# Where the vector and weight work stands at the entry of the recurrence and of the second feed-forward block

## The chip, the core and the metric

The kernel runs on one core of one Trainium2 chip. The metric is the device time of one execution in microseconds (us); the time of a kernel is the median of several runs. Five engines work side by side, each through its own instruction list: TensorE (PE, the matrix products), VectorE (DVE), ScalarE (ACT), GpSimd (POOL) and SyncE (SP, which only starts transfers). They meet through semaphores.

## What is computed

One step of a small audio encoder: 1152 columns (1024 frames of a prompt and 8 streams of 16 frames) by 1024 features, in float32. Two layers, each with a mixer and a feed-forward block:

```python
for i in range(DEPTH):                       # DEPTH = 2
    h = rmsnorm(x, norm_mix_w[i])
    out = conv_module(h, ...) if i == 0 else hgrn2_mix(h, ...)   # hgrn2: gated recurrence
    x = x + out
    h = rmsnorm(x, norm_ffn_w[i])
    x = x + conv_ffn(h, ...)                 # up to 2 x 2816, 3-tap conv, silu gate, down
y = rmsnorm(x, norm_final_w)
# hgrn2_mix: q, f, v, g = split(h @ w_in); f goes through a sigmoid; 8 heads of 128;
# block-wise recurrence per head; normed, gated by silu(g); @ w_o
```

`rmsnorm` divides each column by the root of its mean square over the 1024 features.

## The kernel before, in words

Activations lie by features: `X` is 8 tiles (index m or k) of 128 partitions by 1152 columns. A float32 product is made of three passes over values cut in two: `XH` and `WH` hold rounded high parts, `XL` and `WL` what is left, and a tile product is XH·WH + XL·WH + XH·WL. One output tile of 128 features by 1152 columns is "a product": 8 values of k, three passes, three thirds of 384 columns (`NCH = 3`), so 72 matmuls, each third into a bank of its own of `BANKS` (PSUM). Two sets of three banks take turns; banks 6 and 7 (`MB`) take the column sums.

**Weights.** Each weight unit (128 by 1024) is loaded by SP and cut by POOL (`split(u)`: a touch of one element, L455, a copy to `WH`, L456, a subtraction to `WL`, L458). There are two slots, so `split(u)` waits until the product of unit u-2 is done, and the product of unit u waits for `w_split`.

**A norm at the entry of a block.** `X[m]` becomes final when DVE has added the last product's tile m (`add`, L1341 and L1343). ACT then writes `XH[m]` (`high`, L916) and the square of `X[m]` into one of two `SQ` buffers (L929); DVE writes `XL[m]` (`low`, L1215); POOL adds the square into `ACC` (`square(q0, m)`, L469 and L472). ACT's square m waits until POOL has taken square m-2. After all eight, PE sums `ACC` over features with a matrix of ones (`stats`, L560, three matmuls, one per third), ACT takes the roots (`rms`, L937), DVE their reciprocals (`rstd`, L1223, three of 384 columns). The scale is applied only when a product is read, so the first product of a block runs without it.

**Entry of the recurrence** (unit numbers from `U_HG`). PE makes the products F, Q and V of head 0 (`part`, L671): F in banks 0 to 2, Q in banks 3 to 5, V again in banks 0 to 2, for which DVE must have read F. The statistics stand after two values of k of Q. POOL cuts F's unit, adds all eight squares, then cuts Q's unit. DVE does the three reciprocals, reads F and Q (`projected`, L1496), then clears `SC` and turns the mask, loaded by ACT, to bytes (L1623, L1624).

**Entry of the second feed-forward block.** The eight output tiles of the recurrence (`U_WO` to `U_WO + 7`, PE L883) are added to `X` one after another, one product apart. POOL cuts all eight units and the first of the feed-forward block (`U_F1`), and only then starts on the squares. For this block ACT writes `XH[0]` to `XH[6]` after square 6, since the last output product still reads the old `XH`:

```python
if late is not None and m == KD - 1:
    for k in range(KD - 1):
        act.wait_ge(x_used, late + k + 1)
        high(k)
```

The entry of the first feed-forward block has the same form (eight products L538 of the convolution module's last matrix, then the block), but there POOL's code reads `split(U_PW2 + 2 + m)`, `square(Q_F0, m)` in turn.

Of the kernel before, what the change touches and what calls it, by code (L numbers as in the profile page):

```python
# [5 lines left out]
ALU = mybir.AluOpType  # L6
# [6 lines left out]
P = 128  # L13
# [4 lines left out]
KD = D // P  # L18
# [10 lines left out]
NCH = 3  # L29
# [16 lines left out]
U_HG = U_F0 + FFN_UNITS  # L46
U_WO = U_HG + HG_BIGS
U_F1 = U_WO + KD
# [9 lines left out]
M_N0, M_F0, M_HG = 0, 3, 6  # L58
# [5 lines left out]
Q_N0, Q_F0, Q_HG, Q_F1, Q_FIN = (KD * n for n in range(5))  # L64
# [46 lines left out]
def big_no(what, h):  # L111
    return BIGS.index((what, h))
# [48 lines left out]
def build(nc, d_w, d_x, d_par, d_taps, d_ffp, d_fhist, d_chist, d_state, d_const, d_mask,  # L161
          o_y, o_convp, o_convs, o_hgp, o_hgs, o_ffn):
    with ExitStack() as ctx:  # L163
# [3 lines left out]
        def sem(name):  # L167
            return ctx.enter_context(nc.semaphore(name))
# [3 lines left out]
        XH = sb("XH", [P, KD, T], F32R)  # L172
        XL = sb("XL", [P, KD, T], F32R)
        WRAW = sb("WRAW", [P, 2, 1024])
        WH = sb("WH", [P, 2, 1024], F32R)
        WL = sb("WL", [P, 2, 1024], F32R)
        RSTD = sb("RSTD", [P, T])
# [62 lines left out]
        FG = cut(T, of=HGA)  # L240
# [6 lines left out]
        SC = cut(TCH, P, of=HGA)  # L247
# [3 lines left out]
        VM = cut(NB, P, of=HGA)  # L251
        MASK = cut(LEVELS * P // 4, of=HGA).bitcast(U8).rearrange("p (l c) -> p l c", l=LEVELS)
# [19 lines left out]
        def big_place(what, h):  # L272

            p = 1 if (what, h) == ("Q", 0) else 0
            return PS[:, p * NCH:(p + 1) * NCH, 0:CW]
# [19 lines left out]
        w_split = sem("w_split")  # L295
# [3 lines left out]
        mb_free = sem("mb_free")  # L299
# [7 lines left out]
        mask_in = sem("mask_in")  # L307
# [22 lines left out]
        g_hi = sem("g_hi")  # L330
        g_lo = sem("g_lo")
        a_full, a_free = sem("a_full"), sem("a_free")
        s_full, s_free = sem("s_full"), [sem("s_free0"), sem("s_free1")]
        kept, o_rdy = sem("kept"), sem("o_rdy")
        f_sig = sem("f_sig")
# [7 lines left out]
        def third(k):  # L343
            return slice(k * CW, (k + 1) * CW)
# [21 lines left out]
        def full_big(eng, what, h):  # L366

            eng.wait_ge(a_full, big_no(what, h) + 1)

        def emptied_big(eng, what, h):  # L370

            eng.wait_ge(a_free, big_no(what, h) + 1)
# [67 lines left out]
        @block.gpsimd  # L440
        def _(pool):
            def split(u, i=0, per=0, used=None):


                s = u % 2
                pool.wait_ge(raw_ld[s], lin(i, 8 * per, raw_count(u)))
                if U_HG <= u - 2 < U_WO:
                    pool.wait_ge(a_full, u - 2 - U_HG + 1)
                elif used is None and u >= 2:
                    used = (unit_tile(u - 2) + 1, 0)  # L450
                if used is not None:
                    pool.wait_ge(ps_full, lin(i, used[1], used[0]))

                one = WRAW[:, s, 0:1]
                nc.gpsimd.tensor_tensor(PAD, one, one, ALU.mult)  # L455
                nc.gpsimd.tensor_copy(WH[:, s, :], WRAW[:, s, :]).then_inc(w_hi, 1)  # L456
                pool.wait_ge(w_hi, lin(i, per, u + 1))
                nc.gpsimd.tensor_tensor(WL[:, s, :], WRAW[:, s, :], WH[:, s, :].bitcast(F32),  # L458
                                        ALU.subtract).then_inc(w_split, 1)

            def squares(q0):

                for m in range(KD):
                    square(q0, m)

            def square(q0, m):
                pool.wait_ge(sq_rdy, q0 + m + 1)
                if m == 0:
                    nc.gpsimd.tensor_copy(ACC, SQ[:, 0, :]).then_inc(sq_add, 1)  # L469
                else:  # L470
                    pool.wait_ge(sq_add, q0 + m)
                    nc.gpsimd.tensor_tensor(ACC, ACC, SQ[:, m % 2, :], ALU.add).then_inc(sq_add, 1)  # L472

            def loop(first, times, u, per_u, per_t):

                with pool.Fori(first, times) as i:
                    for k in range(per_u):
                        v = u + k + per_u * first
                        before = unit_tile(v - 2) + 1 - per_t * first
                        assert unit_tile(v - 2 + per_u) + 1 - per_t * (first + 1) == before  # L480
                        split(u + k, i, per_u, (before, per_t))

            def ffn(u0):

                for u in range(u0 + 2, u0 + 7):
                    split(u)
                loop(1, FGROUPS - 1, u0 + 1, 6, 12)
                for u in range(u0 + 1 + 6 * (FGROUPS - 1), u0 + FFN_UNITS):
                    split(u)

            split(0)
            split(1)
            for u in range(U_PW1 + 2, U_PW1 + 6):
                split(u)
            loop(1, (KD - 2) // 2, U_PW1 + 2, 4, 6)
            for u in range(U_PW2 - 2, U_PW2):
                split(u)
            split(U_PW2)
            split(U_PW2 + 1)

            for m in range(KD - 1):
                split(U_PW2 + 2 + m)
                square(Q_F0, m)
            square(Q_F0, KD - 1)
            split(U_F0 + 1)
            ffn(U_F0)

            split(U_HG)
            squares(Q_HG)
            split(U_HG + 1)  # L510
            for u in range(U_HG + 2, U_F1):
                split(u)
            split(U_F1)
            squares(Q_F1)
            split(U_F1 + 1)
            ffn(U_F1)
            squares(Q_FIN)
# [3 lines left out]
        def _(pe):  # L521
# [129 lines left out]
            def part(what, h, k0, k1, lows=None):  # L651

                a = big_no(what, h)
                s = (U_HG + a) % 2
                if k0 == 0:
                    pe.wait_ge(w_split, U_HG + a + 1)
                    if (what, h) == ("F", 0):
                        emptied(pe, T_HG - 2)
                    elif (what, h) == ("Q", 0):
                        emptied(pe, T_HG - 1)  # L660
                    elif (what, h) == ("V", 0):
                        emptied_big(pe, "F", 0)
                    else:
                        pe.wait_ge(a_free, a)
                for k in range(k0, k1):
                    if lows is not None:
                        pe.wait_ge(x_lo, lows + k + 1)
                    wh, wl = WH[:, s, k * P:(k + 1) * P], WL[:, s, k * P:(k + 1) * P]
                    for q, (w, x) in enumerate(((wh, XH), (wh, XL), (wl, XH))):
                        for c in range(NCH):  # L670
                            ins = nc.tensor.matmul(big_place(what, h)[:, c, :], w, x[:, k, third(c)],  # L671
                                                   start=(k == 0 and q == 0), stop=(k == KD - 1 and q == 2),
                                                   skip_group_check=True)
                if k1 == KD:
                    ins.then_inc(a_full, 1)

            def take(what, h):

# [84 lines left out]
                ins.then_inc(s_full, 1)  # L763

            part("F", 0, 0, KD, lows=P_HG)
            part("Q", 0, 0, 2)
            stats(M_HG, Q_HG)
            part("Q", 0, 2, KD)
            part("V", 0, 0, KD)
            scores(0, 0)  # L770
            part("G", 0, 0, 3)
            values(0)
# [136 lines left out]
        def _(act):  # L909
# [23 lines left out]
            def rms(m0):  # L933

                for c in range(NCH):
                    act.wait_ge(mb_full, m0 + c + 1)
                    A(RSTD[:, third(c)], MB[:, (m0 + c) % 2, 0:CW], ACT.Sqrt, bias=EPSC, scale=1.0 / D  # L937
                      ).then_inc(mb_free, 1)
# [159 lines left out]
                act.dma_start(XKEPT[m], X[:, m, :]).then_inc(kept, 16)  # L1098

            split_x(Q_HG, P_HG, C_MIX1, x_kept)  # L1100
            rms(M_HG)

            act.wait_ge(ffn_out, 16)
            act.dma_start(VM, d_mask).then_inc(mask_in, 16)

            def load_state(h):
                act.dma_start(SIN, d_state[h]).then_inc(state_in, 16)
# [90 lines left out]
        def _(dve):  # L1198
# [3 lines left out]
            def mine():  # L1202

                dve.wait_ge(dv, dc.now())
# [14 lines left out]
            def rstd(m0):  # L1219

                for c in range(NCH):
                    dve.wait_ge(mb_free, m0 + c + 1)
                    dc.inc(V.reciprocal(RSTD[:, third(c)], RSTD[:, third(c)]))  # L1223
                mine()
# [266 lines left out]
            def projected(what, h, dst):  # L1491

                full_big(dve, what, h)
                if what == "G":
                    mine()
                V.tensor_tensor(pieces(dst), big_place(what, h), pieces(RSTD[:]), ALU.mult).then_inc(a_free, 1)  # L1496
# [117 lines left out]
                V.tensor_tensor(XL[:, k, :], X[:, k, :], XH[:, k, :].bitcast(F32), ALU.subtract  # L1614
                                ).then_inc(x_lo, 1)

            rstd(M_HG)

            dve.wait_ge(ffn_out, 16)
            projected("F", 0, FG)  # L1620
            projected("Q", 0, QFS[0])
            dve.wait_ge(mask_in, 16)
            dc.inc(V.memset(SC, 0.0))  # L1623
            dc.inc(V.tensor_copy(MASK, VM))  # L1624
            mine()

            forget(0)
            key(0)
# [174 lines left out]
```

## Time and profile before

| | |
|---|---|
| median of 3 runs | 3020.76 us (3020.7 to 3022.45) |
| profiled execution, its own time | 3021.16 us |
| its span, first to last instruction | 3019.4 us |
| PE busy | 2913.8 us, 97% of the span |
| DVE, POOL, ACT busy | 1741.7, 811.1, 522.6 us |
| mean granted TensorE clock | 0.987 of full speed |

The span is 1.8 us shorter than the time of the same execution. PE is busy nearly all of the time; what is left is some 105 us in which it stands still, and stretches with a lower clock.

### The profile page before, as it was taken

Reading aid. Unit: us, or ns where it says so; the run is one execution under the profiler, and the core shown is the slowest. Engines: PE = TensorE matmul, PEld = TensorE weight load, DVE = VectorE, ACT = ScalarE, POOL = GpSimd, SP = SyncE. Lnnn points to the kernel's source line nnn. Section 1 sums busy time; section 2 is a strip of 40 time slices with the busy share of each in tenths; the row PEclk is TensorE's granted clock in tenths of the full one; section 3 lists DMA queues with packets and bytes.
Section 4 is the critical chain, followed back from the end, with each engine's and each line's share of the span. In section 5 each row is a group of like instructions: output and inputs, shape, how many; then the busy total and the mean of one; then the engine's idle time right before and its main releaser. Section 6 shows DMA issues by size and latency. Waiting matters only on the chain. (4 is left out here: it accounts for less than half of the span.)

```text
span 3019.4 us, 41365 instructions
## 1 busy us (share of the span) xinstructions
PE 2913.8 (97%) x16894; PEld 2821.4 (93%) x16894; DVE 1741.7 (58%) x1872; ACT 522.6 (17%) x644; POOL 811.1 (27%) x624
## 2 busy tenths in 40 slices
PE   7999979999999999998999999999899999999996
PEld 6888749999999999998999999989899999999996
DVE  7999971745555555455566555662555555555545
ACT  3011041311111111122111111121211111111121
POOL 3121104322222222225111111112522222222223
PEclk9999989999999999999999999999999999999998
DMA  4001102111111111122110111113011111111111
GB/s 131 25 23 31 26 30 82 43 42 42 42 42 42 42 42 42 42 71 88 43 44 30 37 42 37 43 37 109 32 42 42 42 42 42 42 42 42 43 45 69
DMA packets 63958, 141.40 MB, mean 47 GB/s; under 512 B 22256, under 2 KB 31984, under 8 KB 63856
## 3 DMA queue, kind: packets, MB, share of 16 engines
q1 hardware_dynamic: 36672, 107.49, 10.7%
q10 hardware_dynamic: 27184, 32.49, 3.2%
q8 instruction: 72, 1.18, 0.2%
q14 instruction: 30, 0.25, 0.0%
HBM read 123.89 MB, written 16.07 MB: 46 GB/s over the span
## 5 line engine op out<-in xcount | busy, mean ns | idle before, releaser
L538 PE MATMUL BANKS<-XH,WH 128*128 128x384 f32 x2688 | 617.1, 337 | 41.7 <-DVE XL L1215 21.2
L455 POOL TENSOR_TENSOR SMALL<-WRAW 128x1 f32<-128x1 f32 x196 | 49.4, 252 | 2139.3 <-PE BANKS L538 1525.7
L538 PE MATMUL BANKS<-XL,WH 128*128 128x384 f32 x2688 | 612.5, 335 | 0.0
L538 PE MATMUL BANKS<-XH,WL 128*128 128x384 f32 x2688 | 612.4, 335 | 0.0
L538 PEld LDWEIGHTS BANKS<-XH,WH 128*128 128x128 f32 x2688 | 480.4, 189 | 48.4 <-issue 35.8
L458 POOL TENSOR_TENSOR WL<-WRAW,WH 128x1024 fp32r<-128x1024 f32 x196 | 480.4, 2451 | 15.7
L538 PEld LDWEIGHTS BANKS<-XL,WH 128*128 128x128 f32 x2688 | 481.4, 189 | 0.0
L538 PEld LDWEIGHTS BANKS<-XH,WL 128*128 128x128 f32 x2688 | 481.0, 189 | 0.0
L1341 DVE TENSOR_TENSOR X<-BANKS,X 128x1152 f32<-128x1152 f32 x168 | 228.0, 1357 | 272.7 <-PE BANKS L538 206.5
L1398 DVE SCALAR_TENSOR_TENSOR ARENA<-ARENA 128x1168 f32<-128x1168 f32 x176 | 257.7, 1464 | 130.9 <-ACT ARENA L1041 122.1
L1041 ACT ACTIVATE ARENA<-ARENA 128x1168 f32<-128x1168 f32 x88 | 120.2, 1366 | 942.3 <-DVE ARENA L1237 942.3
L1294 DVE SCALAR_TENSOR_TENSOR X<-ARENA,X (+1 forms) x336 | 266.9, 870 | 0.0
L538 PE MATMUL BANKS<-GH,WH 128*128 128x384 f32 x1056 | 243.5, 338 | 3.1 <-DVE X L1343 1.6
L538 PE MATMUL BANKS<-GL,WH 128*128 128x384 f32 x1056 | 242.8, 338 | 0.0
L538 PE MATMUL BANKS<-GH,WL 128*128 128x384 f32 x1056 | 242.7, 338 | 0.0
L1389 DVE COPY ARENA<-ARENA 128x2 f32 (+1 forms) x88 | 15.1, 172 | 376.4 <-PE BANKS L538 376.3
L456 POOL CAST WH<-WRAW 128x1024 fp32r<-128x1024 f32 x196 | 208.0, 1061 | 0.0
L538 PEld LDWEIGHTS BANKS<-GH,WH 128*128 128x128 f32 x1056 | 189.6, 188 | 5.1 <-DVE X L1341 2.8
L671 PE MATMUL BANKS<-XH,WH 128*128 128x384 f32 x768 | 186.5, 350 | 6.3 <-POOL WL L458 6.0
L538 PEld LDWEIGHTS BANKS<-GH,WL 128*128 128x128 f32 x1056 | 190.1, 188 | 0.0
L538 PEld LDWEIGHTS BANKS<-GL,WH 128*128 128x128 f32 x1056 | 189.9, 188 | 0.0
L671 PE MATMUL BANKS<-XL,WH 128*128 128x384 f32 x768 | 175.5, 336 | 0.0
(138 smaller groups left out, 3231.3 us busy)
## 6 DMA issues: line engine op xcount, KB each, us to landing
WRAW<-in_w SPq DMA_DIRECT2D x188, 512.0 KB, 3.4
X<-in_x SPq DMA_DIRECT2D x8, 576.0 KB, 8.7
X<-in_x ACTq DMA_DIRECT2D x8, 576.0 KB, 8.3
x_kept<-X ACTq DMA_DIRECT2D x8, 576.0 KB, 2.8
X<-x_kept ACTq DMA_DIRECT2D x8, 576.0 KB, 7.8
out_y<-X ACTq DMA_DIRECT2D x8, 576.0 KB, 3.2
HGA<-in_state ACTq DMA_DIRECT2D x8, 512.0 KB, 4.5
out_hgs<-HGA ACTq DMA_DIRECT2D x8, 512.0 KB, 2.6
```

The source lines that it names most:

```text
L455: nc.gpsimd.tensor_tensor(PAD, one, one, ALU.mult)
L456: nc.gpsimd.tensor_copy(WH[:, s, :], WRAW[:, s, :]).then_inc(w_hi, 1)
L458: nc.gpsimd.tensor_tensor(WL[:, s, :], WRAW[:, s, :], WH[:, s, :].bitcast(F32), ALU.subtract).then_inc(w_split, 1)
L538: ins = nc.tensor.matmul(ps_bank(n, c), w, x[:, third(c)], start=(k == 0 and q == 0), stop=(k == last and q == 2), skip_group_check=betwee ...
L671: ins = nc.tensor.matmul(big_place(what, h)[:, c, :], w, x[:, k, third(c)], start=(k == 0 and q == 0), stop=(k == KD - 1 and q == 2), skip ...
L1041: A(C[:, half, 0:CE], U[:, half, 2:EXT], ACT.Identity, bias=CB[:, at], scale=FFP[:, at, FW2:FW2 + 1].rearrange("p a b -> p (a b)")).then_i ...
L1294: dc.inc(V.scalar_tensor_tensor(out=dst, in0=src, scalar=w, in1=dst, op0=ALU.mult, op1=ALU.add))
L1341: ins = V.tensor_tensor(pieces(X[:, m, :]), ps(n), pieces(X[:, m, :]), ALU.add)
L1389: V.tensor_copy(u[:, 0:2], NEGB[:, at].broadcast_to([P, 2]))
L1398: return V.scalar_tensor_tensor(out=c, in0=u[:, k:k + CE], scalar=FFP[:, at, k:k + 1] .rearrange("p a b -> p (a b)"), in1=c, op0=ALU.mult, ...
```

## The change

It touches the entry of the recurrence and that of the second feed-forward block.

- POOL, recurrence: Q's unit is cut after five squares, not eight.
- PE, recurrence: the statistics stand after five values of k of Q, not two; V of head 0 is made bank by bank (`first_values`): all 24 matmuls of a third, then the next third. Each third waits only until that bank of F has been read.
- DVE, recurrence: the clearing of `SC` and the mask come first; then for each third the reciprocal and the reading of that third of F.
- ACT, recurrence: the mask's load is issued ahead of the roots.
- POOL, output product: `square(Q_F1, m)` stands behind `split(U_WO + 2 + m)`, m = 0 to 6, and the last square behind `split(U_F1)`.

```diff
             split(U_HG)
-            squares(Q_HG)
+            for m in range(KD - 3):
+                square(Q_HG, m)
             split(U_HG + 1)
-            for u in range(U_HG + 2, U_F1):
+            for m in range(KD - 3, KD):
+                square(Q_HG, m)
+            for u in range(U_HG + 2, U_WO + 2):
                 split(u)
-            split(U_F1)
-            squares(Q_F1)
+            for m in range(KD - 1):
+                split(U_WO + 2 + m)
+                square(Q_F1, m)
+            square(Q_F1, KD - 1)
             split(U_F1 + 1)
...
+            def first_values():
+
+                a = big_no("V", 0)
+                s = (U_HG + a) % 2
+                pe.wait_ge(w_split, U_HG + a + 1)
+                for c in range(NCH):
+                    if c < NCH - 1:
+                        pe.wait_ge(bank_read, c + 1)
+                    else:
+                        emptied_big(pe, "F", 0)
+                    for k in range(KD):
+                        wh, wl = WH[:, s, k * P:(k + 1) * P], WL[:, s, k * P:(k + 1) * P]
+                        for q, (w, x) in enumerate(((wh, XH), (wh, XL), (wl, XH))):
+                            ins = nc.tensor.matmul(big_place("V", 0)[:, c, :], w, x[:, k, third(c)],
+                                                   start=(k == 0 and q == 0), stop=(k == KD - 1 and q == 2))
+                ins.then_inc(a_full, 1)
...
             part("F", 0, 0, KD, lows=P_HG)
-            part("Q", 0, 0, 2)
+            part("Q", 0, 0, 5)
             stats(M_HG, Q_HG)
-            part("Q", 0, 2, KD)
-            part("V", 0, 0, KD)
+            part("Q", 0, 5, KD)
+            first_values()
...
             split_x(Q_HG, P_HG, C_MIX1, x_kept)
-            rms(M_HG)
-
             act.wait_ge(ffn_out, 16)
             act.dma_start(VM, d_mask).then_inc(mask_in, 16)
+            rms(M_HG)
...
-            rstd(M_HG)
-
             dve.wait_ge(ffn_out, 16)
-            projected("F", 0, FG)
+            dc.inc(V.memset(SC, 0.0))
+            dve.wait_ge(mask_in, 16)
+            dc.inc(V.tensor_copy(MASK, VM))
+            for c in range(NCH):
+                dve.wait_ge(mb_free, M_HG + c + 1)
+                dc.inc(V.reciprocal(RSTD[:, third(c)], RSTD[:, third(c)]))
+                mine()
+                if c == 0:
+                    full_big(dve, "F", 0)
+                V.tensor_tensor(FG[:, third(c)], big_place("F", 0)[:, c, :], RSTD[:, third(c)], ALU.mult
+                                ).then_inc(a_free if c == NCH - 1 else bank_read, 1)
             projected("Q", 0, QFS[0])
-            dve.wait_ge(mask_in, 16)
-            dc.inc(V.memset(SC, 0.0))
-            dc.inc(V.tensor_copy(MASK, VM))
-            mine()
```

The lists of instructions, at the places where this moves them. Each row is a line of the code, the operation, destination and sources, and in brackets the semaphores waited for. First POOL at the entry of the recurrence, before; the L469 and L472 rows are the squares, and the L455 row behind them opens the cut of Q's unit.

```order
L469 COPY ARENA<-ARENA 128x1152 [waits sq_rdy]
L472 TENSOR_TENSOR ARENA<-ARENA 128x1152 [waits sq_add,sq_rdy] x7
L455 TENSOR_TENSOR SMALL<-WRAW 128x1 [waits ps_full,raw_ld1]
L456 CAST WH<-WRAW 128x1024
L458 TENSOR_TENSOR WL<-WRAW,WH 128x1024 [waits w_hi]
```

And of the change (its lines are numbered one higher here):

```order
L470 COPY ARENA<-ARENA 128x1152 [waits sq_rdy]
L473 TENSOR_TENSOR ARENA<-ARENA 128x1152 [waits sq_add,sq_rdy] x4
L456 TENSOR_TENSOR SMALL<-WRAW 128x1 [waits ps_full,raw_ld1]
L457 CAST WH<-WRAW 128x1024
L459 TENSOR_TENSOR WL<-WRAW,WH 128x1024 [waits w_hi]
L473 TENSOR_TENSOR ARENA<-ARENA 128x1152 [waits sq_add,sq_rdy] x3
```

The cut of Q's unit moved ahead of the last three squares. Next DVE from the last two `low` of that entry to the first work on the gates, before:

```order
L1215 SCALAR_TENSOR_TENSOR XL<-X,PAR,XH 128x1152 x2
L1223 RECIPROCAL RSTD<-RSTD 128x384 x3
L1496 TENSOR_TENSOR HGA<-BANKS,RSTD 128x1152 x2
L1623 MEMSET HGA 128x1152
L1624 CAST HGA<-HGA 128x1024
L1501 TENSOR_SCALAR HGA<-HGA,SMALL 128x1152
```

And of the change:

```order
L1235 SCALAR_TENSOR_TENSOR XL<-X,PAR,XH 128x1152 x2
L1638 MEMSET HGA 128x1152
L1640 CAST HGA<-HGA 128x1024
L1643 RECIPROCAL RSTD<-RSTD 128x384
L1647 TENSOR_TENSOR HGA<-BANKS,RSTD 128x384
L1643 RECIPROCAL RSTD<-RSTD 128x384
L1647 TENSOR_TENSOR HGA<-BANKS,RSTD 128x384
L1643 RECIPROCAL RSTD<-RSTD 128x384
L1647 TENSOR_TENSOR HGA<-BANKS,RSTD 128x384
L1516 TENSOR_TENSOR HGA<-BANKS,RSTD 128x1152
```

The clearing and the mask moved ahead of the reciprocals, and the one reading of F became three, each behind its reciprocal. Last POOL at the end of the output product, of the change, from the first of its squares:

```order
L470 COPY ARENA<-ARENA 128x1152
L456 TENSOR_TENSOR SMALL<-WRAW 128x1
L457 CAST WH<-WRAW 128x1024
L459 TENSOR_TENSOR WL<-WRAW,WH 128x1024
L473 TENSOR_TENSOR ARENA<-ARENA 128x1152
```

The last four rows come six times in all, the sixth time with two squares (x2) at the end; before, all these cuts stood one behind another, and all eight squares behind the cut of `U_F1`.

## Rows read from the trace of the kernel before

**Rows 1.** The page, part 1: busy us (share of the span) and instructions.

```profile
PE 2913.8 (97%) x16894; PEld 2821.4 (93%) x16894; DVE 1741.7 (58%) x1872; ACT 522.6 (17%) x644; POOL 811.1 (27%) x624
```

**Rows 2.** Waits of PE: waited for, us in total, times, longest us.

```profile
PE BANKS L538 <- DVE XL L1215: 21.2, 4, 11.5
PE BANKS L671 <- POOL WL L458: 6.0, 1, 6.0
```

**Rows 3.** Timeline of PE, recurrence entry: start us, us, operation [idle before <-releaser].

```profile
1382.38 0.68 PE L671 MATMUL BANKS<-XH,WH 128*128 128x384 f32 x3
...
1390.09 1.33 PE L671 MATMUL BANKS<-XH,WH 128*128 128x384 f32 x3 [5.99 <-POOL WL L458]
...
1394.65 2.39 PE L560 MATMUL BANKS<-ARENA,CONST 128*128 128x384 f32 x6
1396.58 0.98 PE L671 MATMUL BANKS<-XH,WH 128*128 128x384 f32 x3
```

**Rows 4.** Windows of PE: stretch, length, busy, granted clock, DMA share, GB/s.

```profile
1390.00:1393.00 3.00, 2.91 (x9) 0.50 0.57 171
```

**Rows 5.** Timeline of PE, second feed-forward entry.

```profile
2144.34 0.69 PE L883 MATMUL BANKS<-XH,WL 128*128 128x384 f32 x3
2152.74 1.30 PE L538 MATMUL BANKS<-XH,WH 128*128 128x384 f32 x3 [7.72 <-DVE XL L1215]
...
2184.95 0.79 PE L538 MATMUL BANKS<-XH,WH 128*128 128x384 f32 x3 [0.24 <-DVE ARENA L1237]
```

**Rows 6.** Timeline of ACT, second feed-forward entry.

```profile
2137.52 1.17 ACT L929 ACTIVATE ARENA<-X 128x1152 f32<-128x1152 f32 x1 [64.72 <-POOL ARENA L469]
...
2149.78 8.12 ACT L916 ACTIVATE XH<-X,PAR 128x1152 fp32r<-128x1152 f32 x7
```

**Rows 7.** Timeline of PE, first feed-forward entry.

```profile
537.24 0.68 PE L538 MATMUL BANKS<-XH,WH 128*128 128x384 f32 x3
...
549.72 2.39 PE L560 MATMUL BANKS<-ARENA,CONST 128*128 128x384 f32 x6
...
564.44 0.68 PE L538 MATMUL BANKS<-XH,WH 128*128 128x384 f32 x3
```

**Rows 8.** Timeline of POOL, first feed-forward entry.

```profile
516.21 2.67 POOL L472 TENSOR_TENSOR ARENA<-ARENA 128x1152 f32<-128x1152 f32 x1
```

**Rows 9.** Waits of all engines, 2030 to 2260 us.

```profile
DVE X L1341 <- PE BANKS L883: 66.2, 7, 11.1
```

**Rows 10.** Timeline of POOL, recurrence entry.

```profile
1376.38 3.62 POOL L472 TENSOR_TENSOR ARENA<-ARENA 128x1152 f32<-128x1152 f32 x1
...
1386.45 0.19 POOL L455 TENSOR_TENSOR SMALL<-WRAW 128x1 f32<-128x1 f32 x1
...
1387.69 2.34 POOL L458 TENSOR_TENSOR WL<-WRAW,WH 128x1024 fp32r<-128x1024 f32 x1
...
1407.80 4.00 POOL L458 TENSOR_TENSOR WL<-WRAW,WH 128x1024 fp32r<-128x1024 f32 x1
```

**Rows 11.** Timeline of DVE, recurrence entry.

```profile
1374.94 2.51 DVE L1215 SCALAR_TENSOR_TENSOR XL<-X,PAR,XH 128x1152 fp32r<-128x1152 f32 x1
1378.62 2.59 DVE L1215 SCALAR_TENSOR_TENSOR XL<-X,PAR,XH 128x1152 fp32r<-128x1152 f32 x1 [1.17 <-ACT XH L916]
1396.11 7.38 DVE L1223 RECIPROCAL RSTD<-RSTD 128x384 f32<-128x384 f32 x3 [14.89 <-ACT RSTD L937]
1403.52 1.36 DVE L1496 TENSOR_TENSOR HGA<-BANKS,RSTD 128x1152 f32<-128x1152 f32 x1
...
1407.99 1.02 DVE L1623 MEMSET HGA<- 128x1152 f32 x1 [0.19 <-issue]
1408.92 0.63 DVE L1624 CAST HGA<-HGA 128x1024 uint8<-128x1024 f32 x1
...
1412.45 0.76 DVE L1506 TENSOR_SCALAR HGA<-HGA 128x1152 f32<-128x1152 f32 x1
```

**Rows 12.** DMA issues, 1380 to 1420 us: KB each, us to landing.

```profile
HGA<-in_mask ACTq DMA_DIRECT2D x1, 512.0 KB, 3.5
```

More of the change, by code:

```diff
@@ L332, in build @@
         a_full, a_free = sem("a_full"), sem("a_free")
+        bank_read = sem("bank_read")
         s_full, s_free = sem("s_full"), [sem("s_free0"), sem("s_free1")]
@@ L660, in part @@
                         emptied(pe, T_HG - 1)
-                    elif (what, h) == ("V", 0):
-                        emptied_big(pe, "F", 0)
                     else:
```

## The prediction

> **What bounds the kernel now.** I read the page first: PE is busy 97% of the span [rows 1], so the kernel is PE's list plus the places where PE stands still or runs slow. Nothing that another engine does counts unless it moves one of those. The list of PE's waits names them; two of its lines lie at the places of this change [rows 2]. The 6.0 us wait for POOL's L458 is the entry of the recurrence. Of the 21.2 us for L1215 the largest part outside the start of the kernel is a wait of 7.72 us at the second feed-forward entry [rows 5]. Then I read PE's timeline at both places, and at the first feed-forward entry, which has the same work in the order that the change gives to the second.
>
> Recurrence entry. F of head 0 is in its last value of k at 1382.38 [rows 3]. A group of three matmuls takes 0.52 us: the product from 537.24 to 549.72 has 24 of them [rows 7]. So F ends at 1382.38 + 3 x 0.52 = 1383.94, and Q could start there. It starts at 1390.09, when POOL has cut its unit: POOL turned to that unit only at 1386.45, behind the eighth square, and was done at 1387.69 + 2.34 = 1390.03 [rows 10]. After the pause the granted clock is 0.50, the 1.2 GHz level [rows 4].
>
> Second feed-forward entry. The last output product ends at 2144.34 + 0.52 = 2144.86; the first product of the block starts at 2152.74 and the third only at 2184.95 [rows 5]. The cause is upstream: ACT's third square waited 64.72 us for POOL's first, until 2137.52, and the seven writings of `XH` began only at 2149.78 [rows 6]. PE had to wait for the low parts behind them.
>
> **The change, part by part.** (1) Q's unit cut after five squares. The wait and the slow clock go: Q's first two values of k end at 1394.65 [rows 3], 10.71 us after 1383.94, where 6 groups take 3.12. Gain 7.59 us.
>
> Is the cut in time? Square 4 ended just before 1376.38 [rows 10]. A cut takes 1390.03 - 1386.45 = 3.58 us. DVE's `low` 6 ran to 1374.94 + 2.51 = 1377.45 and `low` 7 came at 1378.62 [rows 11]. POOL's square begun at 1376.38 took 3.62 us, against 2.67 with DVE idle [rows 8, 10]: the two engines hold each other up. `low` 7 ended at 1381.21, 1.2 us after that square. So I let the cut wait for `low` 6, and for 1.2 us of `low` 7: 1377.45 + 3.58 + 1.2 = 1382.2. The cleared `SC` now stands right behind `low` 7. At 1407.80 a POOL subtraction took 4.00 us instead of 2.34 while the clearing (1.02) and the mask's cast (0.63) ran [rows 10, 11]; 1.02 more gives 1383.3, still ahead of 1383.94. If the cut goes first instead, `low` 7 ends near 1382.2, and PE wants it at 1382.38. ACT's `high` 7 needs only the squares ahead of the moved cut, so it is not later.
>
> The Trainium skill (SBUF — State Buffer, "Who interferes with whom") says that a DVE instruction with two SBUF inputs and a GpSimd instruction that reads SBUF exclude each other, the first to start holding the port for its whole length. By that rule `low` 7 and the subtraction run one after the other, as 1.2 us behind the square's end suggests, and the sum above stands; without it the cut would end at about 1380 and no square would be late. The page does not count a clearing, which has no input, among the instructions that contend on this chip; the subtraction of 4.00 us says that it does.
>
> (2) Statistics after five values of k. PE is there at 1383.94 + 5 x 1.56 = 1391.74. The three squares left need 3 x 2.8: from 1382.2 they end at 1390.6, from 1383.3 at 1391.7, with the mask's cast in their way at 1392.3. Bounds 0 and 0.6 us of wait; I take 0.2, since the cast must first await ACT's last square and 3.5 us of transfer [rows 12] and may miss the last square.
>
> (3) V by banks, DVE by thirds. The reciprocals started 1396.11 - 1394.65 = 1.46 us after the statistics did [rows 3, 11], so now at 1393.2. Each takes 7.38 / 3 = 2.46 us; reading a third of F costs between 1.36 / 3 = 0.45 and the whole 1.36 [rows 11]. At the upper bound the thirds of F are read at 1397.0, 1400.8 and 1404.7. PE reaches V at 1391.74 + 1.93 (statistics) + 0.30 (the first group behind them takes 0.82) + 3 x 1.56 = 1398.65, and its next banks at 1402.8 and 1407.0: no wait in any case. Without the thirds, V would have waited to about 1402, so this part earns nothing by itself, but part 1 would lose 3 us without it. V's unit is cut from 1392.3 at the latest, in 3.58 to 5.2 us: by 1397.5. What stands behind it: DVE's key of head 0 was done at 1412.45 + 0.76 = 1413.2 [rows 11], with V's end at 1394.65 + 1.93 + 0.30 + 6 x 1.56 + 12.48 = 1418.7. Now Q is read by 1404.7 + 1.36 = 1406.1 instead of about 1407.8, and the 1.65 us of clearing and cast are gone from behind it: the key comes by 1409.9, V ends at 1411.1. The order inside V has the same 72 matmuls and weight loads. New is that neighbours add into one bank. The nearest case is the statistics: six records of 384 columns in 1.93 us, 0.32 each, in pairs that go to one bank [rows 3]. A product's matmul takes 0.173. Bounds for V: 0, and 72 x (0.32 - 0.173) = 10.6 us. I take 0: these records are float32 products, which hold PE twice as long in either bank order, and I see no pause between them.
>
> (4) Squares between the cuts. From the end of the last output product to the start of the third product is 2184.95 - 2144.86 = 40.09 us; at the first feed-forward entry, in the new order, the same stretch is 564.44 - 537.24 = 27.20 us [rows 5, 7]. Gain 12.89 us, the slow clock and the small wait of 0.24 included. On POOL each round holds a cut of 3.58 and a square of 2.67 [rows 8, 10], 6.25 of the 12.48 that a product takes, so no cut comes late. A square waits for DVE's add and ACT's square, and a cut stands behind it. The seven adds waited for PE alone, 66.2 us [rows 9], so the reloaded rows of `X` are there in time.
>
> Sum: 7.59 + 12.89 - 0.2 = 20.3 us. From the profiled execution's 3021.16 (span 3019.4 and 1.8 around it) that leaves 3000.9; the median of before is 0.4 below that execution, so 3000.5.
>
> **The rivals.** A, the recurrence entry gives part back. If the three late squares take 3.62 us each, the value beside DVE, they end 3 x 0.95 = 2.85 later than said, and PE waits up to 3.4 us at the statistics, somewhat more with a clock that falls. For it: every hold-up of [rows 10] falls into this stretch. Against it: DVE has little to do there. Time 3001.5 to 3005.
>
> B, V by banks is slow: 10.6 us at the bound, 3011. Against it: the steady 0.32 of the statistics.
>
> C, the second feed-forward entry keeps its stall, because something other than the squares holds the `XH` back there; only 7.4 is left of the gain: 3013.4. Against it: the first entry, engine for engine the same.
>
> D, slower: POOL stands at a square while PE wants the next unit. Seven rounds hang on this. They eat the whole gain from 20.3 / 7 = 2.9 us of wait each; a round has 6.2 to spare, so DVE's adds would have to come 9.1 us late. Only late reloads could do that, and [rows 9] speaks against it. Time from 3021 up.
>
> **How the numbers follow.** Forecast 0.72 (2999.3 to 3001.5), A 0.19, B 0.03, C 0.03, D 0.03. The likeliest time is 3000.5. The range 2999.0 to 3005.0 takes in the forecast and A; B, C and D stay out. A change of 0.2%, 6 us, is about what can be told from none: forecast, A, B and C are faster, 0.97; D is split, 0.01 within and 0.02 slower.
>
> **What would show it.** PE's 6.0 us wait for POOL's subtraction is gone, and no wait at the statistics over 1 us; the granted clock stays 1.00 around both entries. V's matmuls stand 0.173 apart. POOL's squares lie at 12.5 us intervals through the output product, ACT has no wait of 64.72, and from the last output product's end to the third product of the block it is 27.2 us. A wait of PE for POOL's squares or DVE's reading at the recurrence entry, or a wider spacing in V, would make the prediction wrong by that much.

## The result, and the profile after

The changed kernel takes 2999.71 us (median of 4 runs, 2999.2 to 3000.24) against 3021.11 (3020.7 to 3022.45) for the kernel before on the same chip. The ratio is 0.993, 95% interval 0.9916 to 0.9943. The forecast was 3000.5, with a range of 2999.0 to 3005.0. The profiled execution of the changed kernel took 3000.24 us, its span is 2998.4 us; that is 21.0 us less span than before (3019.4).

The page, part 1 (busy us, share of the span, instructions): PE has the same 16894 matmuls as in [rows 1], and what went is time in which it stood still or ran slow.

```profile
PE 2908.0 (97%) x16894; PEld 2817.4 (94%) x16894; DVE 1737.8 (58%) x1874; ACT 523.0 (17%) x644; POOL 809.2 (27%) x624
```

Waits of PE (waited for, us in total, times, longest us). The 6.0 us for POOL's `WL` of [rows 2] is gone, and so are three of the four waits for the low parts; what is left of that line, 11.5 us, lies at the kernel's start.

```profile
PE BANKS L544 <- DVE XL L1235: 11.5, 1, 11.5
```

Timeline of PE at the recurrence entry (start us, us, operation). L675 is the product by groups of three, L566 the statistics, L694 the new `first_values`, L717 the scores.

```profile
1381.99 0.68 PE L675 MATMUL BANKS<-XH,WH 128*128 128x384 f32 x3
...
1383.55 0.68 PE L675 MATMUL BANKS<-XH,WH 128*128 128x384 f32 x3
...
1391.35 2.39 PE L566 MATMUL BANKS<-ARENA,CONST 128*128 128x384 f32 x6
1393.28 0.98 PE L675 MATMUL BANKS<-XH,WH 128*128 128x384 f32 x3
...
1398.28 0.33 PE L694 MATMUL BANKS<-XH,WH 128*128 128x384 f32 x1
...
1410.59 0.34 PE L694 MATMUL BANKS<-XH,WL 128*128 128x384 f32 x1
1410.76 1.50 PE L717 MATMUL BANKS<-HGA 128*128 128x128 f32 x12
```

The reader is to see that nothing in brackets, that is no wait, stands here. F's last value of k starts at 1381.99 (before 1382.38, [rows 3]), F ends at 1383.55, where Q follows without a pause, the statistics stand 7.80 us behind, which is 5 values at 1.56, and V's 72 matmuls stand 0.173 apart: (1410.76 - 1398.28) / 72.

Timelines of POOL and DVE at the same place. The first POOL row is square 4, then three rows of Q's cut, then squares 5 to 7 in one row. The first two DVE rows are `low` 6 and 7, then the clearing of `SC`, the mask's cast, and the thirds.

```profile
1372.21 3.62 POOL L473 TENSOR_TENSOR ARENA<-ARENA 128x1152 f32<-128x1152 f32 x1
1375.79 1.31 POOL L456 TENSOR_TENSOR SMALL<-WRAW 128x1 f32<-128x1 f32 x1
1377.04 1.04 POOL L457 CAST WH<-WRAW 128x1024 fp32r<-128x1024 f32 x1
1378.16 2.39 POOL L459 TENSOR_TENSOR WL<-WRAW,WH 128x1024 fp32r<-128x1024 f32 x1
1380.50 9.41 POOL L473 TENSOR_TENSOR ARENA<-ARENA 128x1152 f32<-128x1152 f32 x3
```

```profile
1374.54 2.51 DVE L1235 SCALAR_TENSOR_TENSOR XL<-X,PAR,XH 128x1152 fp32r<-128x1152 f32 x1
1378.22 3.54 DVE L1235 SCALAR_TENSOR_TENSOR XL<-X,PAR,XH 128x1152 fp32r<-128x1152 f32 x1 [1.17 <-ACT XH L937]
1381.95 1.02 DVE L1638 MEMSET HGA<- 128x1152 f32 x1 [0.19 <-issue]
1387.64 2.83 DVE L1640 CAST HGA<-HGA 128x1024 uint8<-128x1024 f32 x1 [4.67 <-DMA HGA<-in_mask]
1392.81 2.55 DVE L1643 RECIPROCAL RSTD<-RSTD 128x384 f32<-128x384 f32 x1 [2.33 <-ACT RSTD L958]
1395.40 0.56 DVE L1647 TENSOR_TENSOR HGA<-BANKS,RSTD 128x384 f32<-128x384 f32 x1
...
1401.50 0.56 DVE L1647 TENSOR_TENSOR HGA<-BANKS,RSTD 128x384 f32<-128x384 f32 x1
```

Q's unit is whole at 1378.16 + 2.39 = 1380.55, 3.0 us before PE wants it. The tight place is another one: POOL's subtraction began 0.06 us ahead of `low` 7 and kept it waiting, so `low` 7 took 3.54 us and ended at 1378.22 + 3.54 = 1381.76, 0.23 us before PE came to that value of k. The last of the three squares ends at 1380.50 + 9.41 = 1389.9, 1.4 us before the statistics.

Timelines of PE, POOL and ACT at the second feed-forward entry:

```profile
2136.40 0.68 PE L904 MATMUL BANKS<-XH,WL 128*128 128x384 f32 x3
2136.92 0.68 PE L544 MATMUL BANKS<-XH,WH 128*128 128x384 f32 x3
...
2149.40 2.39 PE L566 MATMUL BANKS<-ARENA,CONST 128*128 128x384 f32 x6
...
2164.14 0.68 PE L544 MATMUL BANKS<-XH,WH 128*128 128x384 f32 x3
```

```profile
2115.89 2.67 POOL L473 TENSOR_TENSOR ARENA<-ARENA 128x1152 f32<-128x1152 f32 x1
2124.75 0.20 POOL L456 TENSOR_TENSOR SMALL<-WRAW 128x1 f32<-128x1 f32 x1 [6.19 <-PE BANKS L904]
...
2128.37 2.68 POOL L473 TENSOR_TENSOR ARENA<-ARENA 128x1152 f32<-128x1152 f32 x1
```

```profile
2126.10 1.17 ACT L950 ACTIVATE ARENA<-X 128x1152 f32<-128x1152 f32 x1 [11.31 <-DVE X L1361]
2127.17 3.54 ACT L937 ACTIVATE XH<-X,PAR 128x1152 fp32r<-128x1152 f32 x3
```

The wait of 64.72 us on ACT and the late writings of `XH` [rows 6] are gone: ACT now waits for DVE's adds, for five of the eight 11.31 us each, the writings begin at 2127.17, and the first product starts at 2136.92, right where the last output product ends. From there to the third product it is 27.22 us, against 40.09 before [rows 5].

**Where the time went.** V of head 0 ends where the scores begin; before, that was here (timeline of PE):

```profile
1418.72 1.50 PE L696 MATMUL BANKS<-HGA 128*128 128x128 f32 x12
```

From F's end to V's end it was 1418.72 - 1383.94 = 34.78 us before and is 1410.76 - 1383.55 = 27.21 now: 7.57. The second feed-forward entry gives 40.09 - 27.22 = 12.87. Another 0.39 us lies ahead of F's last value of k, where nothing was changed: F begins anywhere between 1370.0 and 1371.5 in the profiled executions of this document, a spread that covers it. The 0.2 that is missing to 21.0 was not traced.

### The profile page after: what moved, and what is told of

Same layout as the page of the kernel before. It is cut to its first block and busy times, and to the rows that moved or that the text cites. A ratio compares the mean times of both kernels' runs of the same rounds, so it can differ in the third digit from the quotient of the medians.

```text
span 2998.4 us, 41366 instructions
## 1 busy us (share of the span) xinstructions
PE 2908.0 (97%) x16894; PEld 2817.4 (94%) x16894; DVE 1737.8 (58%) x1874; ACT 523.0 (17%) x644; POOL 809.2 (27%) x624
## 5 line engine op out<-in xcount | busy, mean ns | idle before, releaser
L675 PE MATMUL BANKS<-XH,WH 128*128 128x384 f32 x744 | 180.3, 350 | 0.3 <-issue 0.3
L675 PE MATMUL BANKS<-XL,WH 128*128 128x384 f32 x744 | 169.6, 335 | 0.0
```

## The experiments

Each kernel was timed beside runs of the kernel before on the same chip. The medians of these were 3021.87 (recurrence only, second feed-forward only, V in one, statistics after two), 3021.45 (cut after four, after six, loops bank by bank, two squares first), 3020.96 (the two with late clearing) and 3020.79, one run (the last two). In the diffs `-` and `+` are against the changed kernel, if not said otherwise.

**The two halves apart.** First the recurrence entry alone, with POOL's order at the second feed-forward entry as before:

```diff
-            for u in range(U_HG + 2, U_WO + 2):
+            for u in range(U_HG + 2, U_F1):
                 split(u)
-            for m in range(KD - 1):
-                split(U_WO + 2 + m)
-                square(Q_F1, m)
-            square(Q_F1, KD - 1)
+            split(U_F1)
+            squares(Q_F1)
```

> All of the change except POOL's order through the output product, which is as before. If the two entries gain each for itself, 7.6 us come off before (3021.1): about 3013.5, and PE keeps the wait of 7.7 us for DVE's low part at the second feed-forward entry. Rival: the stall only moves on, and one entry alone gives nearly nothing (3019 or more) or nearly all (3002 or less).

Measured: 3012.87 us (3012.25 to 3013.82), ratio 0.997 (0.9958 to 0.9983), span 3011.5. Then the reverse edit in the kernel before, POOL's new order at the second feed-forward entry alone:

> The kernel before with POOL's squares between the cuts through the output product, nothing else. If the gain of this entry is the stretch from the end of the last output product to the start of the third product of the block, 40.1 down to 27.2 us, the time is 12.9 us under before: about 3008.2. Rival: part of the 12.9 us depends on the recurrence entry: then it and the run with the recurrence part alone don't add up to the 21.4 us of both.

Measured: 3008.32 us (3006.97 to 3008.86), ratio 0.9955 (0.9941 to 0.9969), span 3006.1. Timeline of PE in the first kernel, and its waits in the second: each keeps just the stall that the other half removes.

```profile
2144.85 1.30 PE L542 MATMUL BANKS<-XH,WH 128*128 128x384 f32 x3 [7.73 <-DVE XL L1233]
2148.49 1.33 PE L542 MATMUL BANKS<-XH,WH 128*128 128x384 f32 x3 [0.42 <-DVE XL L1233]
```

```profile
PE BANKS L673 <- POOL WL L458: 6.0, 1, 6.0
```

The spans fall by 7.9 and 13.3 us, together 21.2, where both edits at once take 21.0. The medians fall by 9.0 and 13.5, together 22.5 against 21.4; that is no finer than the kernel before itself, whose runs spread over 2.9 us here. In the trace of the first kernel it is 27.20 us from F's end (1383.59) to the scores (1410.79), as in the change. So the halves do not touch each other, as far as about 1 us can be told.

**V as one product again.** `first_values` is replaced by the product that needs all of F's banks read; DVE still reads by thirds.

```diff
+                    elif (what, h) == ("V", 0):
+                        emptied_big(pe, "F", 0)
...
-            first_values()
+            part("V", 0, 0, KD)
```

> The change, but V of head 0 is made as before, value of k by value of k over three banks, and so waits for all of F's reading; DVE keeps its thirds. In the change V starts at 1398.28 us and the third bank of F is read at 1402.06. If the bank-by-bank form protects the gain of the earlier cut, PE waits 3.8 us here and the time is about 3003.5 to 3004. Rival: V's start doesn't matter because the scores behind it wait for DVE anyway: 2999.7.

Measured: 3005.63 us (3004.95 to 3006.1), ratio 0.9947 (0.9931 to 0.9962), 5.9 above the change. Its timelines of PE, DVE and POOL, and windows of PE (stretch, length, busy, granted clock, DMA share, GB/s):

```profile
1401.77 1.30 PE L677 MATMUL BANKS<-XH,WH 128*128 128x384 f32 x3 [3.77 <-POOL WL L459]
...
1415.64 1.05 PE L719 MATMUL BANKS<-HGA 128*128 128x128 f32 x8
```

```profile
1401.07 0.56 DVE L1649 TENSOR_TENSOR HGA<-BANKS,RSTD 128x384 f32<-128x384 f32 x1
```

```profile
1399.40 2.35 POOL L459 TENSOR_TENSOR WL<-WRAW,WH 128x1024 fp32r<-128x1024 f32 x1
```

```profile
1399.00:1403.00 4.00, 1.23 (x4) 0.78 0.08 11
1403.00:1406.00 3.00, 3.00 (x15) 0.73 0.42 160
```

The row names POOL as the releaser, but POOL had cut V's unit by 1393.5. The subtraction of POOL shown here, which ends at 1399.40 + 2.35 = 1401.75, cuts the next unit, which V does not need: in the change V starts at 1398.28, and that cut ends only at 1402.24. What ended the wait is DVE's third reading of F, done at 1401.07 + 0.56 = 1401.63. The wait is 3.77 us; the prediction had put 3 on it, my expectation 3.8. From the statistics (1390.92 here) to the scores it is 1415.64 - 1390.92 = 24.72 us against 1410.76 - 1391.35 = 19.41 in the change: 5.3 lost. From V's start to the scores it is 1415.64 - 1401.77 = 13.87 us against 12.48: so 1.4 of the 5.3 is the slow clock behind the wait, 0.50 up to 1403 and a mean of 0.73 from 1403 to 1406, where the change runs at 1.00. I had left that out, and the time lies 1.6 us above my 3004.

**Statistics after two values of k, as before the change.** `part("Q", 0, 0, 5)` becomes `part("Q", 0, 0, 2)`, and the rest of Q starts at 2.

> The change, but the statistics stand after two values of k of Q, as before. PE is there 4.7 us earlier, at about 1386.7 us, and the last square ends at 1389.9. If POOL's squares are what the place of the statistics must respect, PE waits about 3.2 us for them, up to 1.5 more with a clock that falls: 3003 to 3004.5. Rival: the place is free: 2999.7.

Measured: 3005.69 us (3003.98 to 3006.39), ratio 0.9945 (0.993 to 0.996). Timeline and windows of PE:

```profile
1390.13 4.21 PE L566 MATMUL BANKS<-ARENA,CONST 128*128 128x384 f32 x6 [3.07 <-POOL ARENA L473]
1393.56 1.74 PE L675 MATMUL BANKS<-XH,WH 128*128 128x384 f32 x3
```

```profile
1391.00:1395.00 4.00, 4.00 (x9) 0.50 0.01 2
```

PE waits 3.07 us for the last square, which ends at 1390.07 (in the change 1389.9). The six float32 matmuls of the statistics then run at half clock: 1393.56 - 1390.13 = 3.43 us where the change needs 1.93. The scores start 33.16 us after Q does, 5.95 later than in the change. The statistics come 1390.13 - 1386.90 = 3.2 of that late (the bracket says 3.07, since the last matmul before them still ends in between), and 2.7 is slow clock. My expectation had allowed 1.5 for it, up to 3004.5. Moving the statistics is thus no detail beside the moved cut: without it most of the 7.6 us is lost again.

**The cut one square earlier, and one later.** In POOL's order `KD - 3` becomes `KD - 4`, or `KD - 2`.

> The change, but Q's unit is cut after four squares, not five. ACT's square 6 waits for POOL's square 4, and high 7 stands behind it, so low 7 comes some 3.5 us later than 1381.8 us, where PE wants it at 1382.0. Expected: a wait of PE for DVE's low part inside F of 2.5 to 3.5 us, time 3002 to 3004. Rival: an earlier cut costs nothing, since the cut has room: 2999.7.

> The change, but Q's unit is cut after six squares. high 7 is free, but the cut ends between 1384.0 and 1385.4 us, the later value if DVE's clearing holds it up, and PE wants it at 1383.55: a wait of PE for POOL's subtraction of 0.5 to 1.9 us, time 3000.2 to 3001.7. Rival: same as the change, 2999.7.

Measured: after four 3004.3 us (3003.22 to 3004.97), ratio 0.9942 (0.9927 to 0.9958); after six 3000.66 (3000.15 to 3001.03), ratio 0.9931 (0.9915 to 0.9946), span 2998.3. Timelines of PE, ACT and DVE with the cut after four, then of PE with the cut after six:

```profile
1384.08 1.33 PE L675 MATMUL BANKS<-XH,WH 128*128 128x384 f32 x3 [2.48 <-DVE XL L1235]
```

```profile
1380.04 1.17 ACT L950 ACTIVATE ARENA<-X 128x1152 f32<-128x1152 f32 x1 [6.16 <-POOL ARENA L473]
```

```profile
1382.39 1.63 DVE L1235 SCALAR_TENSOR_TENSOR XL<-X,PAR,XH 128x1152 fp32r<-128x1152 f32 x1 [4.92 <-ACT XH L937]
```

```profile
1383.40 0.79 PE L675 MATMUL BANKS<-XH,WH 128*128 128x384 f32 x3 [0.65 <-POOL WL L459]
```

A cut that goes too early is no safer. It pushes one of POOL's squares back, ACT's own square waits 6.16 us for that, ACT's writing of `XH` for the last value of k stands behind it (1381.12), and `low` 7 starts at 1382.39, 4.2 us later than in the change. PE waits 2.48 in F and then runs slow (granted clock 0.50 from 1384 to 1386): from its last value of k to the scores it takes 1414.41 - 1384.08 = 30.33 us against 28.77 in the change. That value of k starts 2.65 us late, so 4.2 us are lost in all. One square later PE waits 0.65 us for the cut itself. From F's last value of k (1381.03) to the scores (1410.73) it is 29.70 us, 0.9 more than in the change, and the median is 0.95 higher; the span of the profiled execution is the same because F happened to begin 0.9 us earlier in it. So five squares is the best of the three places, with 0.9 us lost on one side and 4.2 on the other.

**The products of the feed-forward loops bank by bank.** 72 of the large products, those made in the loops of both feed-forward blocks (5184 matmuls), get V's new order.

```diff
+                if per_n == 12:
+                    for c in range(NCH):
+                        for k, (wh, wl, xh, xl) in enumerate(parts):
+                            for q, (w, x) in enumerate(((wh, xh), (wh, xl), (wl, xh))):
+                                ins = nc.tensor.matmul(ps_bank(n, c), w, x[:, third(c)],
...
```

> The change, and the four up products in the loop of both feed-forward blocks are made bank by bank too: 72 products, 5184 matmuls. If neighbours that add into one bank cost nothing, the matmuls stay 0.173 us apart and the time is 2999.7 within 0.2%. Rival: a cost per matmul; at the bound of the prediction, 0.147 us, it is 760 us; already 2 ns each would show as 10 us.

Measured: 2999.7 us (2999.36 to 3000.57), ratio 0.9928 (0.9913 to 0.9943), span 2997.6. The windows of PE from 600 to 700 us, in this kernel and in the change, give one and the same row:

```profile
600.00:700.00 100.00, 100.00 (x575) 1.00 0.13 42
```

Adding 24 times in a row into one bank costs nothing that can be seen in 5184 matmuls. Rival B is out for this size of product.

**Two squares ahead of the first cut**, in the hope of filling PE's 1.6 us wait for `X` ahead of the recurrence:

```diff
+            for m in range(2):
+                square(Q_HG, m)
             split(U_HG)
-            for m in range(KD - 3):
+            for m in range(2, KD - 3):
```

> The change, and POOL adds squares 0 and 1 of the recurrence entry ahead of the cut of F's unit, in the 9.0 us in which it stands idle there. In the change that cut starts at 1355.88 us, holds up DVE's low 2 (3.65 us instead of 1.41), and the add of tile 4 comes late: PE waits 1.6 us for it. If this chain is right, the wait goes and the squares end earlier: about 2998.0. Rival: the wait has another cause, or DVE is held up by the squares instead and PE waits as long elsewhere: 2999.7.

Measured: 3000.78 us (2999.32 to 3000.87), ratio 0.9929 (0.9915 to 0.9942), span 2999.0. Timelines of PE and DVE:

```profile
1363.99 0.79 PE L546 MATMUL BANKS<-GH,WH 128*128 128x384 f32 x3 [1.30 <-DVE X L1365]
...
1367.70 0.80 PE L546 MATMUL BANKS<-GH,WH 128*128 128x384 f32 x3 [0.28 <-DVE X L1365]
```

```profile
1354.40 3.48 DVE L1237 SCALAR_TENSOR_TENSOR XL<-X,PAR,XH 128x1152 fp32r<-128x1152 f32 x1
...
1359.13 3.48 DVE L1237 SCALAR_TENSOR_TENSOR XL<-X,PAR,XH 128x1152 fp32r<-128x1152 f32 x1
```

My expectation failed: 1.6 us of wait became 1.30 + 0.28. The `low` of value 1 is now held up by a square (POOL 1353.97 to 1356.66) and that of value 2 by the subtraction (1358.99 to 1361.39); the order decides which of POOL's instructions stands in DVE's way, not whether one does. The squares did end earlier, at 1377.28 + 10.64 = 1387.9, but nothing waited for them any more.

**Clearing and mask cast, early or late.** In the first kernel both stand behind Q's reading again, in the second the clearing alone.

```diff
-            dc.inc(V.memset(SC, 0.0))
-            dve.wait_ge(mask_in, 16)
-            dc.inc(V.tensor_copy(MASK, VM))
             for c in range(NCH):
...
             projected("Q", 0, QFS[0])
+            dve.wait_ge(mask_in, 16)
+            dc.inc(V.memset(SC, 0.0))
+            dc.inc(V.tensor_copy(MASK, VM))
+            mine()
```

> The change, but VectorE clears the score tiles and casts the mask behind Q's reading again, as before the change; ScalarE still loads the mask early. Theory (the key's chain has slack, so this part of the change only tidies): VectorE's key reading ends near 1406.6 us instead of 1405.0, still ahead of V's last product at 1410.8, so the time is that of the change, 2999.7, within 0.6. Rival (the chain behind V needs both early): the scores start later than 1410.76 and the time is 3001 to 3003. On the clearing: if it holds GpSimd's squares, square 5, which took 3.79 us with low 7 and the clearing beside it, falls to about 2.8; if VectorE's subtraction for low 7 alone holds it, it stays at 3.6 to 3.9.

> The change, but only the clearing of the score tiles stands behind Q's reading; the mask cast stays early. Theory: the cast starts right behind low 7, near 1382, waits for GpSimd's square to end (near 1384.3) and takes as long as that wait plus about 1; the time is that of the change, 2999.7, within 0.6. Rival (the cast, now first, holds GpSimd's square 5 or 6 over 1 us longer, so the statistics wait for the last square past 1391.35): 3000.5 to 3001.5. On the clearing: square 5 stays at 3.6 to 3.9 if the clearing is innocent.

Measured: 2999.44 us (2999.13 to 3000.1), ratio 0.9926 (0.991 to 0.9943), and 2999.95 (2999.54 to 3001.04), ratio 0.9929 (0.9912 to 0.9946). Timelines of DVE, PE and POOL with both late:

```profile
1405.93 0.76 DVE L1526 TENSOR_SCALAR HGA<-HGA 128x1152 f32<-128x1152 f32 x1
```

```profile
1410.61 2.17 PE L717 MATMUL BANKS<-HGA 128*128 128x128 f32 x18
```

```profile
1380.35 9.41 POOL L473 TENSOR_TENSOR ARENA<-ARENA 128x1152 f32<-128x1152 f32 x3
```

The key, which the scores need, is done at 1405.93 + 0.76 = 1406.69, 3.9 us before they start. This part of the change is worth nothing in time. With the clearing alone late, the cast did not start near 1382 as expected: its mask came only at 1387.7, when the squares were nearly done. And the three squares take 9.41 us with the clearing beside them or not, so the clearing does not hold POOL here, against what the prediction had read from the 4.00 us subtraction of [rows 10].

**What then made that subtraction 4.00 us?** Two kernels on that, both from the kernel before: in the first the clearing goes ahead of F's reading, in the second it goes behind the cast.

```diff
             dve.wait_ge(mask_in, 16)
-            dc.inc(V.memset(SC, 0.0))
             dc.inc(V.tensor_copy(MASK, VM))
+            dc.inc(V.memset(SC, 0.0))
             mine()
```

> The kernel before, but VectorE clears the score tiles ahead of F's reading, and only the mask cast is left behind Q's reading, where GpSimd's subtraction took 4.00 us with the clearing (1.02) and the cast (0.63) beside it. Theory (the clearing does not hold GpSimd; the cast alone does): the cast comes right behind Q's reading, within 0.2 us of the subtraction's start, and the subtraction takes 2.34 + 0.2 + 0.6 = about 3.0 to 3.2. Rival (the clearing does hold it): also about 3.0 to 3.2, so this run alone gives only the cast's share; it stands beside the run with the two in the other order. Third case (the subtraction, which starts first, holds the cast): 2.34 and a cast of 2.5 to 3. The time is that of before, 3021, within 1.

> The kernel before, with the mask cast ahead of the clearing, both behind Q's reading. Theory (the clearing does not hold GpSimd): the cast runs first, the subtraction goes on as soon as it ends and takes 3.0 to 3.2 us, with the clearing beside it in 1.02. Rival (the clearing holds it): 4.0 again. If VectorE's work, whatever it is, first waits out a subtraction that started ahead of it, the subtraction takes 2.34. The time is that of before, 3021, within 1.

Measured, one run each: 3021.13 and 3022.32 us (before beside them 3020.79). Timelines of POOL and DVE with the clearing ahead of F's reading:

```profile
1407.76 2.85 POOL L458 TENSOR_TENSOR WL<-WRAW,WH 128x1024 fp32r<-128x1024 f32 x1
```

```profile
1407.67 0.69 DVE L1624 CAST HGA<-HGA 128x1024 uint8<-128x1024 f32 x1
```

and with the clearing behind the cast:

```profile
1408.06 2.86 POOL L458 TENSOR_TENSOR WL<-WRAW,WH 128x1024 fp32r<-128x1024 f32 x1
```

```profile
1407.97 0.69 DVE L1623 CAST HGA<-HGA 128x1024 uint8<-128x1024 f32 x1
1408.84 1.02 DVE L1624 MEMSET HGA<- 128x1152 f32 x1 [0.19 <-issue]
```

Both times lie in the spread of the kernel before (3019.96 to 3022.83 in its other runs), though 3022.32 is more than the 1 us from 3021 that I had allowed. The cast alone adds 0.5 us to 2.34 (it has 0.6 left when the subtraction begins); the clearing behind it adds nothing and is not held either. But with the clearing ahead of the cast, as in [rows 10, 11], the subtraction lasts to 1411.80. That is 2.25 us after the end of the cast (1409.55), and in the two new kernels it is 2.25 and 2.26: each time the subtraction ends about one plain length (2.34) behind the cast. So it was held to the end of the cast, although the cast began 1.12 us after it. That the queued cast has a claim on the port before it starts would explain it; that is argued, and no run shows it apart. Nor has any run a clearing that starts beside a subtraction with no cast behind it, so that the clearing took the port there and handed it to the cast isn't ruled out for this one place. In the changed kernel the cast stands behind a wait for the mask, and no such row occurs.

## Why the prediction was right

**Q's unit cut after five squares: 7.59 forecast, 7.57 measured** from F's end to V's end, with no loss at the statistics. The cut was ready at 1380.55 instead of my 1382.2: 1.2 us because POOL's subtraction was issued 0.06 us ahead of `low` 7 and held it, not the other way round, and 0.4 because the whole stretch lay 0.4 earlier. That was my second branch ("if the cut goes first instead, `low` 7 ends near 1382.2, and PE wants it at 1382.38"); `low` 7 ended at 1381.76 and PE came at 1381.99. The slack was as thin as that branch said, 0.2 us, and on the other engine than my main line had it. That nothing was lost here hung on those 0.2 us, and is in part luck. The Trainium skill (SBUF — State Buffer, "Who interferes with whom") says that of two such instructions the first issued holds the shared port for its whole length: the trace agrees, with 3.54 us for `low` 7 behind a subtraction that runs its plain 2.39, and 3.79 for square 5, which begins 1.26 us before `low` 7 ends.

**Statistics after five values: 0.2 forecast, 0 measured.** The squares ended at 1389.9, ahead of my 1390.6 to 1392.3, since the cut was earlier. The mask's cast did not delay them; it was held itself by the last square and took 2.83 us instead of 0.63. The step was needed, as the sum assumed: with the statistics after two values the kernel loses 6.0.

**V by banks, DVE by thirds: 0 forecast, 0 measured.** V's 72 matmuls took 12.48 us, as in the old order. The third reading of F ended at 1402.06, before the bound of 1404.7, and PE wanted that bank at 1398.28 + 2 x 4.16 = 1406.6. That the old order would cost part 1 "3 us" was too low: the wait is 3.77, and the slow clock behind it makes 5.3. The clock stood at nothing in this term; in my expectation for the statistics after two values it was there, but at up to 1.5 us instead of 2.7.

**Squares between the cuts: 12.89 forecast, 12.87 measured.** The rounds are those of the first feed-forward entry, as taken: a cut of 3.6 us, a square of 2.67, 6.19 us of waiting for PE.

**The sum.** 20.3 us were forecast, and the span fell by 21.0: 7.57 + 12.87, the 0.4 ahead of F's last value of k, and 0.2 not traced. The price of 0.2 for the statistics did not come. The measured 2999.71 lies 0.8 below the forecast.

**What was wrong in the text** is the clearing: I let it hold POOL for 1.02 us, on the 4.00 us row. It did not: with and without it the three squares take 9.41 us. The page of the Trainium skill named above says that a DVE instruction with at most one SBUF input, outside the modes with two ports, does not contend with GpSimd. The traces agree in three places: the clearing took 1.02 us beside a square (the change), beside a cast of POOL that took its plain 1.04 (cut after six squares) and beside the subtraction with the mask's cast first. The subtraction of 4.00 us itself is the one place where this stays open. In the sum this only widened the bounds.

**The rivals.** A needed three squares of 3.62 us; one took 3.79 and two 2.67. B is out by V's 12.48 us and by 5184 matmuls more, C by the third product at 27.22 us. D did not occur: each of POOL's waits in those rounds is for PE, none at a square but the last, where nothing is behind it that PE wants yet.

## What to carry to other kernels

When a unit of work is moved forward on one engine, follow what it pushes back on the same engine to every engine that waits for that: here one square too early cost 4.2 us and one too late 0.9, the first because ACT's and DVE's last part hung on the square. Where PE must wait, price the wait and the slow clock behind it together: waits of 2.5 to 3.8 us here cost 1.4 to 2.7 us more. And a change of several parts is best priced with each taken out once: without the place of the statistics 6.0 of the 7.6 us were lost, without V by banks 5.3, without the early clearing and cast nothing. The cut itself was only moved by one square, not taken out.

## What the runs showed of the hardware

- After waits of 2.48, 3.77 and 3.07 us TensorE ran at a granted clock of 0.50, the lower level of 1.2 GHz, and lost 1.6, 1.4 and 2.7 us from there to the scores. The largest loss is the one where the float32 statistics fell into the slow stretch. After waits of 0.65, 1.30 and 0.28 us the granted clock stayed 1.00; the next group of three took 0.63 us instead of 0.52 or 0.53, and little more was lost.
- The order of two instructions of VectorE, a clearing and a cast, decides how long a subtraction on GpSimd beside them takes: 4.00 us with the clearing first, 2.86 with the cast first. In both it ends 2.25 us after the cast does.
- The releaser that the profile names can be wrong when a product waits for two things: for a wait that VectorE's reading ended it named GpSimd, whose cut of the unit needed was done 8 us earlier, while another unit's cut ended 0.02 us before the wait did.
